# Query norm moved into the softmax of a hybrid attention / S5 / expert trunk step, with packed sums of squares and one modulation step moved inside each tile

## The reference, cut to what matters

```
q = rmsnorm(z[..., :D_ATTN].reshape(B, L, N_HEADS, HEAD_DIM), p['q_norm'])
k = rmsnorm(z[..., D_ATTN:2*D_ATTN].reshape(...), p['k_norm'])
s_loc = einsum(q, k) * HEAD_DIM**-0.5 + bias     # masked 2-D window
s_ctx = einsum(q, k_ctx) * HEAD_DIM**-0.5
pr = softmax(concatenate([s_loc, s_ctx]))
o  = pr @ [v, v_ctx]
```

## Time and profile before

| | |
|---|---|
| median of 3 runs | 2447.45 us (2444.28 to 2448.87) |
| the profiled execution's own time | 2447.0 us |
| its span in the profile | 2445.2 us |
| granted TensorE clock over the span | 0.979 of full speed |
| PE busy | 2283.5 us (93%) |
| DVE, ACT, POOL busy | 749.2, 494.9, 590.6 us (31%, 20%, 24%) |
| heads with their modulation steps | about 484 to 1036 us |
| experts | from about 1400 us to the end |

### The profile page before, as it was taken

One profiled execution on the slowest core, in us unless ns is written; L12 is line 12 of the kernel. 1 busy time (PEld: TensorE's weight loads), 2 busy tenths in 40 slices (PEclk: granted clock), 3 DMA queues, 4 the chain that ended last, 5 costly groups with the idle time before them and its releaser, 6 DMA issues.

```text
span 2445.2 us, 57164 instructions
## 1 busy us (share of the span) xinstructions
PE 2283.5 (93%) x25836; PEld 1506.6 (62%) x25836; DVE 749.2 (31%) x1119; ACT 494.9 (20%) x1027; POOL 590.6 (24%) x644
## 2 busy tenths in 40 slices
PE   5999999999999999999999489999999999999997
PEld 3468888655555555654445476666766666666663
DVE  4124432477777777320124400000000000000001
ACT  3011111355655565310012100000000000000000
POOL 0246770556666566000200100000000000000000
PEclk9999999999999999999998599999999999999999
DMA  9922223854646463332423789999999999999995
GB/s 370 359 76 74 71 52 75 221 194 147 197 159 208 159 197 107 133 121 77 165 121 137 258 331 391 411 413 411 415 409 411 408 411 409 410 405 393 408 415 188
DMA packets 182973, 630.81 MB, mean 258 GB/s; under 512 B 13002, under 2 KB 89508, under 8 KB 152324
## 3 DMA queue, kind: packets, MB, share of 16 engines
q1 hardware_dynamic: 164224, 587.07, 62.7%
q0 software_dynamic: 3328, 20.97, 3.2%
q10 hardware_dynamic: 15188, 19.19, 2.3%
HBM read 602.75 MB, written 24.44 MB: 257 GB/s over the span
## 4 chain that ended last, share of the span: by engine, by line
PE 69%; DMA 12%; DVE 9%; ACT 4%; issue 3%; SPq 1%; ACTq 1%; POOL 0%; DVEq 0%; POOLq 0%
PE PS L1549 19%; PE PS L1459 11%; PE PS L1563 10%; PE PS L1379 9%; PE PS L1193 7%; DMA work<-in_w_gate 6%; DMA hT_<-in_w_gate 5%; PE PS L1135 3%; DVE PS L1898 3%; PE PS L1070 2%; DVE work L1866 2%; ACT work L964 1%; PE PS L1097 1%; DMA work<-in_w_ada 1%; DVE small L1844 1%
## 5 line engine op out<-in xcount | busy, mean ns | idle before, releaser
L1549 PEld LDWEIGHTS PS<-hT_,work 128*64 128x64 f32 x14336 | 511.1, 139 | 85.6 <-issue 68.0
L1549 PE MATMUL PS<-hT_,work 128*64 128x80 f32 x14336 | 530.1, 235 | 28.0 <-issue 19.5
L1379 PE MATMUL PS<-hT_,work 128*128 128x512 f32 (+1 forms) x1536 | 435.1, 435 | 2.5 <-DVE work L1871 2.5
L2145 POOL TENSOR_TENSOR work<-work 128x512 f32<-128x512 f32 x240 | 305.0, 1271 | 195.3 <-ACT work L964 181.9
L1379 PEld LDWEIGHTS PS<-hT_,work 128*128 128x128 f32 x1536 | 226.1, 191 | 151.7 <-issue 147.5
L1563 PE MATMUL PS<-work,hT_ 128*32 128x512 f32 (+1 forms) x2544 | 300.9, 596 | 9.3 <-DMA work<-in_w_down 5.8
L2009 DVE TENSOR_TENSOR hT_<-PS,hT_ 128x480 f32<-128x480 f32 x16 | 10.5, 658 | 933.0 <-ACT hT_ L1053 933.0
L1459 PE MATMUL PS<-work,mixT_ 128*128 128x512 f32 x640 | 280.7, 599 | 0.0
L2199 POOL DMA_INDIRECT out_y<-mixT_,work x16 | 23.4, 1461 | 795.2 <-DVE mixT_ L2027 795.2
L1459 PEld LDWEIGHTS PS<-work,mixT_ 128*128 128x128 f32 x640 | 122.3, 193 | 149.6 <-issue 149.6
L1193 PE MATMUL PS<-work,hT_ 128*128 128x256 f32 x960 | 212.9, 380 | 1.4 <-DMA work<-in_w_in 1.4
(11 more groups left out here) (261 smaller groups left out, 1925.9 us busy)
## 6 DMA issues: line engine op xcount, KB each, us to landing
work<-in_w_up SPq DMA_DIRECT2D x57, 2048.0 KB, 25.8
work<-in_w_down SPq DMA_DIRECT2D x56, 2048.0 KB, 31.2
work<-in_w_gate SPq DMA_DIRECT2D x55, 2048.0 KB, 30.7
work<-in_w_ada SPq DMA_DIRECT2D x48, 2048.0 KB, 9.8
work<-in_w_in SPq DMA_DIRECT2D x80, 512.0 KB, 6.4
hT_<-in_w_gate SPq DMA_DIRECT2D x9, 2048.0 KB, 31.3
work<-in_w_out SPq DMA_DIRECT2D x4, 4096.0 KB, 14.2
hT_<-in_w_down SPq DMA_DIRECT2D x8, 2048.0 KB, 29.9
```

The lines of the kernel that those rows point to most:

```text
L1379: last = pe.matmul(qk_bank(which)[:, (ctx_at if ctx_ else lat_at)[which]], w_chunk[chunk % NW][:, HD * (k % 8):HD * (k % 8) + HD], hT[:, k ...
L1549: last = pe.matmul(hidden_at(u, f)[64 * h:64 * h + 64, :], w[:, k % 4, f // 2, f % 2, 64 * h:64 * h + 64], xsT[s][:, k, :], start=opens, s ...
L2145: TT_(acc_ctx[p % 3], acc_ctx[p % 3], prod[i % 3], ALU.add).then_inc(s_padd, 1)
```

## The change

It touches the heads alone, and computes the same function.

- **Query norm.** The queries are no longer multiplied by their reciprocal root. ACT writes them times the gain alone into `qT` (`gained`), directly behind their squares. The bias is multiplied by the root of the row (`query_rms`) before it is added to the unnormed scores, and the exponential applies `query_scale`, the reciprocal root, as its scale for each row. The maximum is multiplied by the same factor before it is the exponential's bias (`scaled_max`), one small DVE instruction for each tile.
- **Sums of squares of queries.** Four products with 32 columns of ones each, one for each quarter of the tokens, write four column groups: 160 columns on 128 partitions in place of 640. DVE transposes 32x32 blocks of this (`query_sums_turned`), so that a token's sum stands in its own partition, five columns for five tiles.
- **Roots.** ACT takes the 128x5 root of the queries together with the keys' root (`roots`), at the start of the next step; the queries' two large roots are gone, and so are DVE's two reciprocals of 320 columns and its 640-column product. DVE's `normed` has one 128x5 reciprocal more.
- **Modulation steps on DVE.** In each slot 0 to 4 of DVE one `late` step now stands between the maximum and the wait for the exponentials. The steps between slots become fewer by as many.

```diff
+        query_rms, query_scale, scaled_max = small[:, 40:45], small[:, 48:53], small[:, 56:58]
+        turned_sums = sq[0][:, 0:TT * 32].rearrange("p (k i) -> p k i", k=TT)[:, :, 0]
...
 # ACT
-                    act.activation(probs[b][:, 64:64 + w], bank(6, w), ACT.Exp, bias=small[:, 2 + b:3 + b],
-                                   accum_out=small[:, 4 + b:5 + b]).then_inc(s_ex, 1)
+                    act.activation(probs[b][:, 64:64 + w], bank(6, w), ACT.Exp, bias=scaled_max[:, b:b + 1],
+                                   scale=query_scale[:, k:k + 1], accum_out=small[:, 4 + b:5 + b]).then_inc(s_ex, 1)
...
             def squares(h, which):
+                if h and not which:
+                    act.wait_ge(s_root, 2 * h)
                 act.activation(sq[which], qk_bank(which), ACT.Square).then_inc(s_sq, 1)
-            def root(h, which):
-                act.wait_ge(s_ss, 2 * h + which + 1)
-                if which:
-                    act.wait_ge(s_qn, h + 1)
-                elif h:
-                    act.wait_ge(s_kn, h)
-                act.activation(rstd[:, lat_at[which]], bank(4), ACT.Sqrt, bias=eps[:, :], scale=1 / HD)
-                act.activation(rstd[:, ctx_at[which]], ctx_sums(which), ACT.Sqrt, bias=eps[:, :], scale=1 / HD)\
-                    .then_inc(s_root, 1)
+            def gained(h):
+                act.activation(qT[h % 2], qk_bank(0), ACT.Identity, scale=q_gain[:, :]).then_inc(s_qn, 1)
+            def roots(h):
+                act.wait_ge(s_root, 2 * h + 1)
+                act.activation(query_rms, turned_sums, ACT.Sqrt, bias=eps[:, :], scale=1 / HD)
+                act.wait_ge(s_ss, 2 * h + 2)
+                act.activation(rstd[:, lat_at[1]], bank(4), ACT.Sqrt, bias=eps[:, :], scale=1 / HD)
+                act.activation(rstd[:, ctx_at[1]], ctx_sums(1), ACT.Sqrt, bias=eps[:, :], scale=1 / HD).then_inc(s_root, 1)
...
 # ACT, step
-                    root(g, 1)
+                    roots(g)
...
                     squares(h, 0)
+                    gained(h)
...
-                    root(h, 0)
...
 # PE (sums becomes sums_free with the waits, query_sums and key_sums)
+                for q in range(4):
+                    last = pe.matmul(bank(4)[32 * q:32 * q + 32, 0:TT * 32], ones[:, 0:32],
+                                     sq[0].rearrange("p (k q i) -> p q k i", k=TT, q=4)[:, q], start=True, stop=True)
+                last.then_inc(s_ss, 1)
...
 # DVE, slot
-                        ch.link(TT_(bank(6, 256), bank(6, 256), biasm[gs][:, VARIANT[k], :], ALU.add))
-                    dve.tensor_reduce(small[:, 2 + b:3 + b], bank(6, w), AX, ALU.max, negate=True).then_inc(s_mx, 1)
+                        ch.link(STT(bank(6, 256), biasm[gs][:, VARIANT[k], :], query_rms[:, k:k + 1], bank(6, 256),
+                                    ALU.mult, ALU.add))
+                    ch.link(dve.tensor_reduce(small[:, 2 + b:3 + b], bank(6, w), AX, ALU.max, negate=True))
+                    TS_(scaled_max[:, b:b + 1], small[:, 2 + b:3 + b], query_scale[:, k:k + 1], None, ALU.mult).then_inc(s_mx, 1)
...
+                if between is not None:
+                    late(g + 1, between, 1)
...
-            def query_root(h, half):
-                if h < HEADS:
-                    dve.wait_ge(s_root, 2 * h + 1)
-                    cols = slice(half * TOK // 2, (half + 1) * TOK // 2)
-                    ch.link(dve.reciprocal(rstd[:, cols], rstd[:, cols]))
-            def query_normed(h):
-                if h < HEADS:
-                    STT(qT[h % 2], qk_bank(0), q_gain[:, :], rstd, ALU.mult, ALU.mult).then_inc(s_qn, 1)
+            def normed(h):
+                dve.wait_ge(s_root, 2 * h + 2)
+                ch.mark(dve.reciprocal(query_scale, query_rms))
+                ch.link(dve.reciprocal(rstd, rstd))
+                STT(kT[h % 2], qk_bank(1), k_gain, rstd, ALU.mult, ALU.mult).then_inc(s_kn, 1)
+            def query_sums_turned(h):
+                if h < HEADS:
+                    dve.wait_ge(s_ss, 2 * h + 1)
+                    dve.transpose(sq[0][:, 0:TT * 32], bank(4, TT * 32)).then_inc(s_root, 1)
...
 # DVE, step
-                late(h, 0, 3)
-                for k in range(3):
-                    slot(g, k)
-                    late(h, 3 + 3 * k, 3)
-                slot(g, 3)
-                query_root(h, 0)
-                late(h, 12, 3)
-                slot(g, 4)
-                query_root(h, 1)
+                late(h, 0, 1)
+                slot(g, 0, 1)
+                late(h, 2, 3)
+                slot(g, 1, 5)
+                late(h, 6, 2)
+                slot(g, 2, 8)
+                late(h, 9, 2)
+                slot(g, 3, 11)
+                query_sums_turned(h)
+                late(h, 12, 2)
+                slot(g, 4, 14)
                 late(h, 15, 3)
                 slot(g, 5)
-                query_normed(h)
```

More of the change, by code:

```diff
@@ L1384, in part, with sums_free @@
                         last.then_inc((s_qmm, s_kmm)[which], 1)
-            def sums(h, which):
+            def sums_free(h, which):
                 pe.wait_ge(s_sq, 2 * h + which + 1)
@@ L1392, in sums, with query_sums, key_sums @@
                     pe.wait_ge(s_late_row, rows)
-                pe.matmul(bank(4), ones, sq[which][:, lat_at[which]], start=True, stop=True)
-                pe.matmul(ctx_sums(which), ones, sq[which][:, ctx_at[which]], start=True, stop=True).then_inc(s_ss, 1)
+            def query_sums(h):
+                sums_free(h, 0)
+                for q in range(4):
+                    last = pe.matmul(bank(4)[32 * q:32 * q + 32, 0:TT * 32], ones[:, 0:32],
+                                     sq[0].rearrange("p (k q i) -> p q k i", k=TT, q=4)[:, q], start=True, stop=True)
+                last.then_inc(s_ss, 1)
+            def key_sums(h):
+                sums_free(h, 1)
+                pe.matmul(bank(4), ones, sq[1][:, lat_at[1]], start=True, stop=True)
+                pe.matmul(ctx_sums(1), ones, sq[1][:, ctx_at[1]], start=True, stop=True).then_inc(s_ss, 1)
             def late_sums(h, end):
@@ L1424, in step @@
                 if g >= 0:
-                    sums(g, 1)
+                    key_sums(g)
                 part(h, 0, False, range(2, 8))
@@ L1438, in step @@
                 part(h, 1, False, range(0, 3))
-                sums(h, 0)
+                query_sums(h)
                 context_key(h)
@@ L1467, in _ @@
             out_tile(0, 0, others[0:3])
-            sums(last_head, 1)
+            key_sums(last_head)
             out_tile(0, 0, others[3:])
@@ L1830, in _, with slot @@
             dve.memset(probsT_half, 0.0).then_inc(s_padz, 1)
-            def slot(g, k):
+            def slot(g, k, between=None):
                 if g < 0:
+                    if between is not None:
+                        late(g + 1, between, 1)
                     return
@@ L1853, in slot @@
                         .then_inc(s_pn, 1)
-            def normed(h, which):
-                dst, gain, done = ((qT, q_gain[:, :], s_qn), (kT, k_gain, s_kn))[which]
-                dve.wait_ge(s_root, 2 * h + which + 1)
+            def normed(h):
+                dve.wait_ge(s_root, 2 * h + 2)
+                ch.mark(dve.reciprocal(query_scale, query_rms))
                 ch.link(dve.reciprocal(rstd, rstd))
-                STT(dst[h % 2], qk_bank(which), gain, rstd, ALU.mult, ALU.mult).then_inc(done, 1)
-            def query_root(h, half):
+                STT(kT[h % 2], qk_bank(1), k_gain, rstd, ALU.mult, ALU.mult).then_inc(s_kn, 1)
+            def query_sums_turned(h):
                 if h < HEADS:
-                    dve.wait_ge(s_root, 2 * h + 1)
-                    cols = slice(half * TOK // 2, (half + 1) * TOK // 2)
-                    ch.link(dve.reciprocal(rstd[:, cols], rstd[:, cols]))
-            def query_normed(h):
-                if h < HEADS:
-                    STT(qT[h % 2], qk_bank(0), q_gain[:, :], rstd, ALU.mult, ALU.mult).then_inc(s_qn, 1)
+                    dve.wait_ge(s_ss, 2 * h + 1)
+                    dve.transpose(sq[0][:, 0:TT * 32], bank(4, TT * 32)).then_inc(s_root, 1)
             def late_rows(h, end):
@@ L1902, in step @@
                 if g >= 0:
-                    normed(g, 1)
+                    normed(g)
                 late_rows(h, False)
-                late(h, 0, 3)
-                for k in range(3):
-                    slot(g, k)
-                    late(h, 3 + 3 * k, 3)
-                slot(g, 3)
-                query_root(h, 0)
-                late(h, 12, 3)
-                slot(g, 4)
-                query_root(h, 1)
+                late(h, 0, 1)
[9 more added lines that the diff above has]
+                slot(g, 4, 14)
                 late(h, 15, 3)
                 slot(g, 5)
-                query_normed(h)
                 late(h, 18, 3)
```

## The result

The changed kernel takes 2413.47 us (median of 4 runs, 2411.67 to 2415.27) against 2447.77 us (4 runs, 2444.28 to 2448.87): a ratio of 0.9869, with a 95% interval of 0.9855 to 0.9882. The profiled execution took 2412.53 us, its span is 2410.7 us. The forecast was 2412 us, with a range of 2404 to 2424.

What follows compares the result with a forecast made beforehand. PE was taken to bound the heads. From 2447.0 us, 29.8 of waits and 8.2 of query sums come off and 3.0 stays at tile 3: 2412.0, or 2412.4 on the median; forecast 2412 us, range 2404 to 2424.

Steps and rivals of the forecast that it cites:

- what bounds: In the heads PE sets the pace, busy 94 of 100 us; DVE or ACT work matters only where PE waits.
- the whole 29.8 us: All PE waits for DVE or ACT in the heads, from 484 to 1036 us, counted as removed with the query norm.
- not added, only moved: DVE's modulation steps, moved between maximum and wait for exponentials: no cost where the exponential follows at once, up to 0.75 us otherwise.
- what is late next: Tile 3: its exponential on ACT stands behind modulation steps 12 to 14, and step 14 needs POOL's addition 11.
- rival B: Tile 3's exponential becomes the new wait at its old height, POOL's three additions binding ACT: 2420 us, chance 0.14.
- the remainder: Waits left at tile 3: 0.3 us in each of ten steps with modulation, 3.0 us; bounds 0 and 11 us.
- A: The forecast itself, with 0 to 0.5 us of tile 3's wait left: 2406 to 2416 us, chance 0.70.
- the packed sums: Query sums on PE in four column groups take 0.4 us instead of 1.08, 12 x 0.68 = 8.2 us off PE's path.
- at most 0.10 us: Drain of PE at a tiling-mode change, taken to fit in the packed stretch's 0.10 us beyond streaming; at most that lost again.
- the squares and `gained` ahead of tile 2's maximum: On ACT they end at 859.5, the maximum is ready at 859.6 to 859.8: just covered, otherwise up to 0.3 us.
- any wait at tiles 0 to 2: Sign of being wrong: a PE wait appearing for tiles 0 to 2 in the heads.
- Rival D: Slower: the chain from scores to probabilities binds at tiles 3 and 4, held by ACT through POOL; 2459 us, chance 0.06.

Runs made afterwards that it cites:

- experiment 4: The changed kernel with one unused 128x1 root more on ACT before modulation step 12, bringing back two table loads: 2427.38 us, ratio 0.9916.
- experiment 6: The changed kernel with two unused 128x320 reciprocals more on DVE, before modulation steps 12 and 15, in eleven steps: 2432.82 us, ratio 0.9949.
- experiment 3: The changed kernel with DVE's modulation steps back in threes between the slots, none between a maximum and its reciprocal: 2422.25 us, ratio 0.9892.
- experiment 7: The kernel before, reordered: ACT's query root behind slot 3 and DVE's two reciprocals behind slot 4: 2463.88 us, ratio 1.0069.
- experiment 1: The changed kernel with tile 3's exponential on ACT put ahead of modulation steps 12 to 14: 2410.2 us, ratio 0.9849.
- experiment 5: The changed kernel with tile 3's exponential ahead of modulation steps 12 to 14 and tile 4's ahead of 15 to 17: 2404.73 us, ratio 0.9823.
- experiment 2: The changed kernel with the query sums at all 128 columns of ones, without column groups (norm left wrong): 2414.03 us, ratio 0.9859.
- experiment 8: The changed kernel with tiles 3 and 4's exponentials ahead on ACT and query sums without column groups: 2408.62 us, ratio 0.9842.

## Why the prediction was right, and which terms were off

**Right: what bounds, and where the waits come from.** PE sets the pace, and four of the five kinds of wait come back with the norm's work. Each half was put back alone: the table loads cost 13.9 us (experiment 4, at tile 3), the reciprocals 19.4 us (experiment 6, at tile 4, the modulation's sum and the output's copy), both with a part that is the clock's. The wait for the normed queries, 2.5 us, has no run of its own; its product is gone. The two prices are each taken from the changed kernel and are not shares of the gain: with the 8.8 us of experiment 3 they come to 42.1, against 34.3 won, and no run has both halves back. The one other order that was tried in the kernel before was slower (experiment 7).

**Missing: the move of DVE's modulation steps.** I counted the whole 29.8 us as the norm's, and the steps as "not added, only moved". Experiment 3 is the change without that move, and 13.9 us of waits stay in place of 7.3. The move took away 6.6 us of them and was worth 8.8 us of time.

**Right: what is late next.** Tile 3's exponential, behind POOL's additions, as rival B's mechanism and as the remainder of A. The 7.3 us of waits lie half-way between A's 3.0 and B's 11. Experiments 1 and 5 show the mechanism: two moves of order on ACT empty the wait.

**Mis-sized: the remainder.** I put 3.0 us, it was 7.3, of the same ten steps (0.63 to 0.81 us) and two of 0.18 at tile 1. The addition was off in two places. Shifted by the 25.48 us between the two steps' key blocks, the exponential starts at 867.5 instead of 866.9. That begins at tile 2: its maximum, scaled, is there at 834.95, shifted 860.4, and I had 859.6 to 859.8; in this step DVE was late, since its product at tile 1 (830.91) had taken 1.22 us beside an addition of POOL. And the product at tile 3 takes 1.20 us where I took 0.42 to 0.88: its row in the kernel before was one sample of a duration that depends on when it meets an addition. PE's own side was right: it wants the probabilities at 843.3, shifted 868.8 as forecast.

**Mis-sized: the packed sums.** 0.41 us against 0.4 expected, which looks exact, but the gain is 0.52 us for each head and not 0.68, so 6.2 us and not 8.2, because the packed products and what follows them start 0.16 us later (experiments 2 and 8). In the kernel before the same stretch, from the key blocks to the block behind the sums, is 862.59 - 858.83 = 3.76 us, against 3.25. This is the place where the rule of "TensorEngine Tiling (Array Packing)", Key Properties, in the Trainium skill applies, that a change of mode drains the engine. I let it pass as at most 0.10 us within the packed stretch; it shows at its borders. That a drain is the cause fits the rows, and no run isolates it.

**Not additive.** The sum took waits and PE's own work as separate terms. In the changed kernel they are one: without the packing the time is the same within 0.6 us (experiment 2), since tile 3's time is set elsewhere. The packing pays only once that wait is gone (experiment 8).

**Missing: what a wait costs beside its idle time.** The stage fell by 37.1 us. Waits account for 29.8 - 7.3 = 22.5 and the sums for 6.2. The other 8.4 us go with 30 waits fewer (42 to 12), 0.28 us each, or 0.22 without the clock's part below. Other pairs give the same: from the changed kernel to experiment 5, 9.2 us of stage, 6.9 us of waits, ten waits fewer, 0.23 us each; to experiment 1, 1.1 us for five. The rows show how. The profile counts as idle only what lies behind a product's modelled end, but without a wait the next product starts ahead of that end. In experiment 5 nothing waits at tile 3:

```profile
836.63 0.38 PE L1346 MATMUL PS<-work 128*128 128x128 f32 x2
836.86 0.49 PE L1077 MATMUL PS<-consts,work 128*128 128x128 f32 x3
```

The transposes start 0.23 us behind the scores there, and 1.19 us behind them in the changed kernel (843.11 to 844.30). That is 0.96 us for a wait that counts as 0.81, and the three transposes then take 0.06 us longer. Before the scores of tile 4 it is the same: 3.82 us from the projection's start in the earlier trace rows and 3.44 in the changed kernel, 0.38 us for a wait of 0.22, and the scores hold PE for 0.49 us instead of 0.38. About 1.7 us of the 8.4 is the granted clock, which was 0.79 from 576 to 584 us in the kernel before, around a wait of 1.84 us, and 1.00 in the changed one. None of my terms had this price of a wait in it.

These errors cancel: -22.5 - 6.2 - 8.4 = -37.1 in the heads against -35.0 forecast, and 2.6 us of scatter and shift elsewhere. The forecast took 4.3 us too little for the remainder and 2.0 too much for the sums, and missed 8.4. That it came within 1.5 us of the median is luck in that part; that PE's waits were what the change gives back was not.

**Right, small.** The bias at 0.490 us (0.47 taken), the scaled maximum 0.214 (0.2), the transposition 0.338 (0.35), the squares and `gained` ahead of tile 2's maximum: PE waits for none of them at tiles 0 to 2, save 0.18 us at tile 1 twice, behind a product of 1.2 us. I had named any wait at tiles 0 to 2 as a sign of being wrong; at 0.4 us in all it was not one. Rival D's outcome did not come: tile 4's delay was DVE's (experiment 6), though ACT, through POOL, does hold tile 3 as D had it.

## What to carry to other kernels

When a wait of the bounding engine is removed, look for the next thing that stands ahead of the same operand, on every engine that feeds it: here it was three modulation steps in ACT's order, tied to POOL, and moving two lines was worth 8.7 us more. Savings on the bounding engine are worth nothing at a point where it waits for another; take out the wait first, then the work. In this kernel a short wait of TensorE cost its idle time and some 0.25 us more, and a packed product cost its neighbours' start: count both. Work that has to be done anyway can stand in the wait for an exponential; price that move by itself. An instruction that was long in one row may only have met another engine's.

## What the runs showed of the hardware

- The product of 128x384 in SBUF on DVE took 0.42 us. If an addition of POOL was running at its start, it ended 0.22 us behind that addition (1.20 us in all at tile 3); as a scalar_tensor_tensor 0.62 us, or 0.42 us behind the addition (1.41 us). DVE's modulation steps, which have PSUM among their operands, took 0.75 us throughout.
- Four column groups of 32 ran side by side at 160 columns too: 0.41 us for eight instructions, against 1.09 us with full width, with 0.16 us lost at the borders.
- A short wait of PE cost 0.22 to 0.28 us beside the idle time that the profile gives it; for one wait the rows give 0.81 us of idle time and 1.02 us of delay.
- In experiment 7 the granted clock was at its lower level (0.50) from 793 to 795 us, right behind a wait of PE of 4.0 us, a mean of 0.79 over 8 us, and 0.96 over the heads. Of the three waits of 1.84 us in the kernel before it fell at the first alone: 0.79 from 576 to 584 us, and 1.00 around the two others.
